# Retention operands 1536 bytes apart, head ends in two parts, and splits moved between engines, in a float32 two-layer trunk

## The chip, the cores and the metric

The kernel runs on one NeuronCore of a Trainium2 chip. The metric is device time in microseconds (us) of one execution; lower is better. Five engines work side by side, each with its own instruction stream, and meet at semaphores: TensorE (PE) multiplies, VectorE (DVE), ScalarE (ACT) and GpSimd (POOL) work on elements, SyncE (SP) issues the weight transfers. PEld is TensorE's weight load.

## The reference

The trunk is two layers over 256 tokens plus 16 meta tokens, so T = 272 columns, with D = 2048:

```python
for layer in range(DEPTH):                       # DEPTH = 2
    u = rmsnorm(h, mix_norm_pre[layer])
    u = hybrid_mixer(u, ...) if layer % 2 == 0 else retention_mixer(u, ...)
    h = h + rmsnorm(u, mix_norm_post[layer])
    u = swiglu(rmsnorm(h, ffn_norm_pre[layer]), w_gate, w_up, w_down)
    h = h + rmsnorm(u, ffn_norm_post[layer])
return h[:, N_META:]

def retention_mixer(h, w_in, w_out):             # 8 heads, q/k 256 wide, v and gate 512 wide
    q, k, v, gate = _split(h @ w_in, RET_IN_SIZES)
    q = _rotate_pairs(q, pos); k = _rotate_pairs(k, pos) * C_QK_DIM ** -0.5
    o = _rms(_chunk_retention(q, k, v))
    return (jax.nn.silu(gate) * o) @ w_out
```

The change touches mostly the product `h @ w_in` of the retention layer and what follows it head by head.

## The kernel before

**Products.** Activations lie transposed: 16 blocks (k) of 128 features in the partitions, tokens along the row. A weight piece is 128 output features times 2048 input features, 1 MB, and gives one output tile. Each float32 number is kept as a high and a low part (`x_hi`, `x_lo`, `w_hi`, `w_lo`, type float32r), and a product of one k is three matmuls, hi·hi, lo·hi and hi·lo, so 48 matmuls a piece. In each of them the weights are the stationary operand (128 by 128) and x is the moving one, 272 columns wide, or 256 where the meta tokens are not needed.

**Making a piece.** SP loads it into `raw` (two slots). ACT copies it to `w_hi` in two halves of 1024 columns (L1501), DVE subtracts to get `w_lo` (L2229, again two halves), and SP may load the slot anew. PE waits for `lo_ready`.

**Where the operands lie.** In bytes from the start of a partition's row, the built program has `x_hi` at 18560, `x_lo` at 35968, `w_hi` at 87200, `w_lo` at 103712, and `mid` and `y_hi` (which share a place) at 143712, `y_lo` at 161120. Weight blocks of successive k are 512 bytes apart. For x there are two layouts, both in `x_of`. With t0 = 0 the rows of successive k are 272 words, 1088 bytes, apart. With t0 = 16, used by the FFN of layer 1, they are 256 words, 1024 bytes, apart and start 56 words (X_FRONT) into the tensor. Retention takes the first layout, also for its pieces of 256 columns, which skip the first 16 words of each row. The activations of the down product of layer 0 lie in `mid`, 2560 bytes apart, the low part 1152 bytes behind the high one (`mid_at`).

**Retention.** `ret_round(i)` is a head: 12 pieces s, q (s = 0, 1; 256 columns), k (2, 3) and v (4 to 7) of 272, gate (8 to 11) of 256. Head 0 is different: its first three pieces are multiplied together while x is still being made (`fresh_three`), all of head 0's first eight with 272 columns. DVE takes each tile out of PSUM; POOL finishes the rotation (L3223, L3224) from `rot_a`. At a head's end `ret_finish` runs on DVE at step s = 0 of the next head: two multiplications of 128 by 1024 (L2984, L2988), then it waits for ACT's high part (L2157), then subtracts the low part (L2994). Only behind these does DVE take tile 0 and split piece 2. Small tensors of the heads (scores, v, gate) are carved out of `u`.

**Openings.** An opening is the start of up0, ret_in and up2 (norms 2, 4 and 6): DVE updates h two blocks at a time (L2314, L2320) and makes `x_lo` (L2305), ACT makes `x_hi`, POOL adds squares (L3075), and PE follows block by block with three pieces at once, of which one sits in `third_hi`/`third_lo` and a fourth waits in `fourth_raw`. Amid the blocks, behind k = 7, DVE also splits the second half of piece 1.

Of the kernel before, what the change touches and what calls it, by code (L numbers as in the profile page):

```python
# [26 lines left out]
F32R = mybir.dt.float32r  # L27
# [4 lines left out]
P = 128  # L32
D = 2048
# [144 lines left out]
def trunk(nc, a, out):  # L178
    ctx = ExitStack()
    st = stage_table()  # L180
    with ctx:
# [7 lines left out]
        h = sb("h", [P, KC, T])  # L189
        x_hi = sb("x_hi", [P, KC, T], F32R)  # L190
# [77 lines left out]
        with ExitStack() as second:  # L268
# [20 lines left out]
            ret_r = sb("ret_r", [P, SEQ], F32, second)  # L289
            ones_ret = sb("ones_ret", [P, P], F32R, second)  # L290
# [23 lines left out]
        sum_hi, sum_lo = third_hi[:, 0:SEQ], third_hi[:, SEQ:2 * SEQ]  # L314
# [4 lines left out]
        def carve(cursor, shape):  # L319

            n = int(np.prod(shape[1:]))
            part = flat[0:shape[0], cursor[0]:cursor[0] + n]
            cursor[0] += n
            assert cursor[0] <= KC * T
# [28 lines left out]
        rel = carve(c4, [P, REL_W])  # L353
        dmask = carve(c4, [P, REL_W])
        ret_s = carve(c4, [P, REL_W])
        v_rows = carve(c4, [P, 2, 512])
        v_tail = carve(c4, [P, 4, 32])
        v_tail_rows = carve(c4, [P, P])
        v_t = carve(c4, [P, T])
        ret_g = carve(c4, [P, 4, SEQ])  # L360
# [135 lines left out]
        def _(sp):  # L496
# [103 lines left out]
            load_third("up2", a["w_up"][4 * HALF + 2])  # L600
            with sp.Fori(0, KC) as i:
                for s in range(2):
                    load(s, FULL, a["w_ret_out"][ds1(2 * i + s)], base + 2 * i + s)
# [27 lines left out]
        def _(pe):  # L631
# [58 lines left out]
            def fresh_hi(norm, k, t0):  # L690
# [3 lines left out]
                mm(o, w_hi[:, 0, k * P:(k + 1) * P], x_of(x_hi, t0)[:, k], k == 0, False)  # L694
                mm(o, w_lo[:, 0, k * P:(k + 1) * P], x_of(x_hi, t0)[:, k], False, False)

            def fresh_lo(norm, k, t0):

                pe.wait_ge(x_lo_ready, KC * (norm // 2) + k + 1)
                return mm(ps[:, BK_0, t0:T], w_hi[:, 0, k * P:(k + 1) * P], x_of(x_lo, t0)[:, k],  # L700
# [29 lines left out]
            def fresh_three(stage, norm, t0):  # L730
# [3 lines left out]
                for k in range(KC + 2):  # L734
# [5 lines left out]
                    if 0 <= j < KC:  # L740
                        if j % 8 == 0:
                            pe.wait_ge(lo_ready, 2 * (base + 1) + 1 + j // 8)
                        pair = multiply(ps[:, BK_1, t0:T], 1, j, 1, lambda _: x_of(x_hi, t0)[:, j],
                                        lambda _: x_of(x_lo, t0)[:, j], j == 0, j == KC - 1)
# [4 lines left out]
                    if n >= 0:  # L749
# [3 lines left out]
                        mm(o, third_hi[:, cut], x_of(x_hi, t0)[:, n], n == 0, False)  # L753
                        mm(o, third_hi[:, cut], x_of(x_lo, t0)[:, n], False, False)
                        last = mm(o, third_lo[:, cut], x_of(x_hi, t0)[:, n], False, n == KC - 1)
# [483 lines left out]
            def mix(n, k0, k1):  # L1239

                piece, _, tile, _ = LAST_AT[f"mix{n}"]
                if k0 == 0:
                    open_tile(piece, tile)
                last = multiply(ps[:, tile % 2, 0:T], piece % 2, k0, k1 - k0, lambda k: y_hi[:, EARLY_K[k0 + k]],
# [20 lines left out]
            gdn_y(g, 1)  # L1265

            pe.wait_ge(FV.sem, FV.after("y_lo", g - 1))
            mix(0, 10, 12)
# [139 lines left out]
            def ret_tile(i, s, t0=0, behind=None):  # L1408
# [5 lines left out]
                multiply(ps[:, s % 2, t0:T], s % 2, 0, KC, lambda k: x_hi[:, k, t0:T], lambda k: x_lo[:, k, t0:T],  # L1414
# [74 lines left out]
        def _(act):  # L1489
# [85 lines left out]
            def fill_x(norm, loaded, after=None):  # L1575
# [3 lines left out]
                def high(k):  # L1579
                    nc.scalar.activation(x_of(x_hi, t0)[:, k], h[:, k, t0:T], ACT.Copy, scale=gains[:, norm, k:k + 1]  # L1580
                                         ).then_inc(x_hi_ready, 1)
# [300 lines left out]
            def mixer_body(i, g, f, d):  # L1882
# [75 lines left out]
                index_pair(i, 14)  # L1958
                index_pair(i, 15)
                gdn_v(g, 2)  # L1960
# [34 lines left out]
            split_last("mix0", EARLY_W, (0,))  # L1995
# [12 lines left out]
            split_last("mix2", EARLY_W)  # L2008
            dsa_exp(5)
            gdn_y(g, 1)  # L2010
# [14 lines left out]
            split_last("mix5", EARLY_W)  # L2025
            dsa_exp(6)
            gdn_y(g, 6)
# [1303 lines left out]
```

## Time and profile before

| | us |
|---|---|
| median of 3 runs | 2899.7 (2899.48 to 2899.88) |
| the profiled execution | 2899.09 |
| its span, first to last instruction | 2897.3 |
| PE busy | 2868.1 (99%) |
| DVE / ACT / POOL busy | 1697.0 / 1367.4 / 233.8 |
| mean granted TensorE clock | 0.999 of full speed |

The span starts with the first instruction of the program; what lies around it is 1.8 us in this execution. A matmul's end is modelled, so its duration reads as 0.28 us while the next one starts after 0.11 to 0.13 us: what a matmul costs here is read from the distance between starts, that is from the length of an unbroken stretch divided by its matmuls. "Idle" of an engine is the time before an instruction in which it did nothing, and the name behind it is what ended that.

### The profile page before, as it was taken

The page shows a single profiled execution, that of the slowest core. Times are in us where ns is not written, and L with a number is a line of the kernel's source. Part 1 is how long each engine was busy: PE and PEld are TensorE (multiplying, and loading weights), DVE is VectorE, ACT ScalarE, POOL GpSimd, SP SyncE. Part 2 cuts the span into 40 slices and gives each one's busy share as a digit, 9 for nine tenths or more (in the row PEclk, how much of TensorE's full clock was granted, in tenths as well). Part 3 has the DMA queues.
Part 4 walks back from the last instruction along what each step waited for, and adds up shares of the span by engine and source line. Part 5 has one row for each costly group of instructions (what it writes and reads, how often), then busy time and mean ns, then how long its engine had stood idle before and what let it go on. Part 6 is the DMA issues. An engine that isn't in the chain of part 4 may idle for free.

```text
span 2897.3 us, 58388 instructions
## 1 busy us (share of the span) xinstructions
PE 2868.1 (99%) x22720; PEld 2796.0 (97%) x22720; DVE 1697.0 (59%) x2404; ACT 1367.4 (47%) x1996; POOL 233.8 (8%) x270
## 2 busy tenths in 40 slices
PE   9999999999999999999999999999999999999998
PEld 8889999999999999999999999999999998899987
DVE  5887775755554555546555555554456556655555
ACT  5556665643333333345544444444454444344443
POOL 2122110200000000001211111110010000000000
PEclk9999999999999999999999999999999999999999
DMA  5222334444445544455444444445544555555554
GB/s 213 102 98 88 124 104 140 163 156 176 176 164 175 183 174 174 176 179 176 145 164 170 165 166 161 169 164 189 190 174 167 193 188 210 196 189 188 189 202 160
DMA packets 74823, 483.89 MB, mean 167 GB/s; under 512 B 8989, under 2 KB 9417, under 8 KB 24432
## 3 DMA queue, kind: packets, MB, share of 16 engines
q1 hardware_dynamic: 74528, 482.30, 46.8%
q8 instruction: 59, 0.97, 0.1%
q0 software_dynamic: 208, 0.39, 0.0%
q14 instruction: 28, 0.23, 0.0%
HBM read 480.41 MB, written 2.10 MB: 167 GB/s over the span
## 4 chain that ended last, share of the span: by engine, by line
PE 90%; DVE 6%; ACT 2%; issue 2%; DMA 0%; POOL 0%; DVEq 0%; SPq 0%; ACTq 0%; POOLq 0%
PE ps L633 89%; DVE w_lo L2378 1%; DVE w_lo L2229 1%; DVE x_lo L2305 1%; DVE ps L2314 0%; DVE h L2320 0%; PE ps L1024 0%; DVE conv_acc L2407 0%; PE ps L1423 0%; ACT w_hi L1501 0%; DMA h<-in_x_t 0%; DVE bias L2509 0%; DVE kq L2421 0%; DVE ret_sq L2988 0%; DVE u L2984 0%
## 5 line engine op out<-in xcount | busy, mean ns | idle before, releaser
L633 PE MATMUL ps<-x_hi,w_hi 128*128 128x272 f32 (+1 forms) x4944 | 1422.4, 288 | 6.7 <-ACT x_hi L1580 3.3
L633 PE MATMUL ps<-x_hi,w_lo 128*128 128x272 f32 (+1 forms) x4944 | 1403.1, 284 | 0.2 <-DVE u L2644 0.2
L633 PE MATMUL ps<-x_lo,w_hi 128*128 128x272 f32 (+1 forms) x4944 | 1400.3, 283 | 2.5 <-DVE x_lo L2305 2.3
L2229 DVE TENSOR_TENSOR w_lo<-raw,w_hi 128x1024 fp32r<-128x1024 f32 (+2 forms) x889 | 1006.9, 1167 | 374.3 <-ACT w_hi L1501 359.5
L1501 ACT ACTIVATE w_hi<-raw 128x1024 fp32r<-128x1024 f32 (+2 forms) x835 | 821.0, 1012 | 506.0 <-PE ps L633 428.3
L633 PEld LDWEIGHTS ps<-x_hi,w_hi 128*128 128x128 f32 x4944 | 931.9, 188 | 14.4 <-issue 6.5
L633 PEld LDWEIGHTS ps<-x_lo,w_hi 128*128 128x128 f32 x4944 | 931.5, 188 | 6.2 <-DVE x_lo L2305 4.9
L633 PEld LDWEIGHTS ps<-x_hi,w_lo 128*128 128x128 f32 x4944 | 927.7, 188 | 0.7 <-DVE u L2644 0.5
L633 PE MATMUL ps<-mid,w_hi 128*128 128x272 f32 (+1 forms) x2432 | 437.1, 282 | 0.0
L633 PEld LDWEIGHTS ps<-mid,w_hi 128*128 128x128 f32 x2432 | 374.3, 188 | 0.0
L633 PE MATMUL ps<-mid,w_lo 128*128 128x272 f32 (+1 forms) x1216 | 342.7, 282 | 0.0
L633 PEld LDWEIGHTS ps<-mid,w_lo 128*128 128x128 f32 x1216 | 227.9, 187 | 0.0
L633 PE MATMUL ps<-w_hi,mid 128*128 128x512 f32 x704 | 218.9, 392 | 0.0
L2119 ACT ACTIVATE mid<-ffn_m 128x272 f32 (+3 forms) x88 | 37.3, 424 | 345.4 <-DVE ffn_m L2956 345.4
L633 PEld LDWEIGHTS ps<-w_hi,mid 128*128 128x128 f32 x704 | 132.0, 188 | 29.5
L2133 ACT ACTIVATE ffn_g<-ffn_g 128x272 f32<-128x272 f32 (+1 forms) x88 | 37.4, 425 | 228.6 <-DVE ffn_g L2944 228.6
L633 PE MATMUL ps<-w_lo,mid 128*128 128x512 f32 x352 | 138.5, 393 | 0.0
L633 PE MATMUL ps<-u 91*91 91x91 f32 (+8 forms) x928 | 110.1, 255 | 3.1 <-DVE state L2649 1.1
L2952 DVE TENSOR_TENSOR ffn_m<-ps,r_pre 128x272 f32<-128x272 f32 (+1 forms) x88 | 38.0, 432 | 124.2 <-PE ps L633 124.2
L633 PEld LDWEIGHTS ps<-u 91*91 91x91 f32 (+4 forms) x928 | 95.9, 158 | 9.5 <-DVE state L2649 1.6
L1548 ACT ACTIVATE sq<-u 128x272 f32<-128x272 f32 (+3 forms) x48 | 20.4, 425 | 145.3 <-DVE u L2354 75.8
L633 PEld LDWEIGHTS ps<-w_lo,mid 128*128 128x128 f32 x352 | 66.1, 188 | 15.3
(362 smaller groups left out, 2355.8 us busy)
## 6 DMA issues: line engine op xcount, KB each, us to landing
raw<-in_w_up SPq DMA_DIRECT2D x172, 1024.0 KB, 4.8
raw<-in_w_ret_in SPq DMA_DIRECT2D x94, 1024.0 KB, 4.8
raw<-in_w_down SPq DMA_DIRECT2D x64, 704.0 KB, 4.0
raw<-in_w_rows SPq DMA_DIRECT2D x44, 1024.0 KB, 4.8
raw<-in_w_heads SPq DMA_DIRECT2D x32, 1024.0 KB, 4.8
raw<-in_w_ret_out SPq DMA_DIRECT2D x32, 1024.0 KB, 4.8
raw<-in_w_mix_early SPq DMA_DIRECT2D x16, 768.0 KB, 4.3
raw<-in_w_latent SPq DMA_DIRECT2D x6, 1024.0 KB, 4.8
```

What stands on the lines that cost most here:

```text
L633: return nc.tensor.matmul(o, lhs, rhs, start=start, stop=stop)
L1501: nc.scalar.activation(w_hi[:, piece % 2, cut], raw[:, piece % 2, cut], ACT.Copy).then_inc(hi_ready, count)
L1548: nc.scalar.activation(sq[:, slot, t0:T], src[:, ds1(k), t0:T], ACT.Square).then_inc(squared, 1)
L2119: nc.scalar.activation(mid[:, bass.ds(mid_at(layer, False, j), w)], ffn_m[:, slot, 0:w], ACT.Copy).then_inc(mid_hi_ready, 1)
L2133: nc.scalar.activation(ffn_g[:, s, 0:w], ffn_g[:, s, 0:w], ACT.Silu).then_inc(gate_silu, 1)
L2229: V.tensor_tensor(w_lo[:, slot, cut], raw[:, slot, cut], w_hi[:, slot, cut], ALU.subtract).then_inc(lo_ready, count)
L2305: V.scalar_tensor_tensor(x_of(x_lo, t0)[:, ds1(k)], h[:, ds1(k), t0:T], gains[:, norm, ds1(k)], x_of(x_hi, t0)[:, ds1(k)], ALU.mult, ALU.s ...
L2378: done = V.tensor_tensor(w_lo[:, s % 2, cut], raw[:, s % 2, cut], w_hi[:, s % 2, cut], ALU.subtract)
L2952: V.tensor_tensor(ffn_m[:, s, 0:w], ps[:, up_bank, t0:T], r_pre[:, t0:T], ALU.mult).then_inc(drained, 1)
```

## The change

1. In retention x has a layout of its own: a tensor `ret_x` over the place of `x_hi`, `x_lo` and `u`, rows of successive k 384 words (1536 bytes) apart, the first at word 40, the low part 16 rows behind. The 272 columns start at byte 18720 + 1536k, the last 256 of them 64 bytes later.
2. What was carved out of `u` for the heads now lies in `h_rows`, the place of `third_hi` and `third_lo`. So the table `rel` is fetched by POOL after the three pieces of the opening, and the third piece of up2 is loaded in the middle of ret_out and no longer at its start.
3. `ret_finish` keeps the two multiplications; the low part is a new `ret_rest`, at s = 1. In head 0 the k tile goes to `rot_b`, in the place of `ret_sq`, and doesn't wait for POOL.
4. In openings POOL subtracts the second half of piece 1 (`split_second`), and no longer DVE. In the first rounds of the FFN, ACT's copy and DVE's split of the piece at slot 1 are made one tile earlier.
5. In the mixer of layer 0 some splits and copies change places, and piece mix0 is made in pieces of 512 and 1024 columns.

```diff
+            ret_x = sb("ret_x", [P, 3 * KC * T], F32R, spaced)
+        RET_FRONT, RET_STEP = 40, 384
-        def x_of(x, t0):
+        def x_of(x, t0, norm=None):
+            if norm == 4:
+                w0 = RET_FRONT + (KC * RET_STEP if x is x_lo else 0)
+                return ret_x[:, w0:w0 + KC * RET_STEP].rearrange("p (c t) -> p c t", c=KC)[:, :, 0:T]
...
-                multiply(ps[:, s % 2, t0:T], s % 2, 0, KC, lambda k: x_hi[:, k, t0:T], lambda k: x_lo[:, k, t0:T],
+                multiply(ps[:, s % 2, t0:T], s % 2, 0, KC, lambda k: x_of(x_hi, 0, 4)[:, k, t0:T],
+                         lambda k: x_of(x_lo, 0, 4)[:, k, t0:T],
...
+            def split_second(stage):
+                piece = st[stage][0] + 1
+                cut = slice(HALF_W, FULL)
+                pool.wait_ge(hi_ready, 2 * piece + 2)
+                pool.wait_ge(lo_ready, 2 * piece + 1)
+                G.tensor_tensor(w_lo[:, 1, cut], raw[:, 1, cut], w_hi[:, 1, cut], ALU.subtract).then_inc(lo_ready, 1)
...
-                        if k == 6:
-                            split_lo(1, FULL, piece, 1)
+                    dve.wait_ge(lo_ready, 2 * piece + 2)
...
-                    if s == 0 and not (isinstance(i, int) and i == 0):
+                    if s == 1 and not (isinstance(i, int) and i == 0):
                         ret_y(i - 1)
...
                     if s == 0 and not first:
                         ret_finish(i - 1)
+                    if s == 1 and not first:
+                        ret_rest(i - 1)
...
+                        to = rot_b if s == 2 and first else rot_a
+                        V.tensor_tensor(to[:, 0, t0:T], tile, rope[:, 0, t0:T], ALU.mult)
...
-                            if not first:
-                                split_next(f"up{n}", i, 4 if opened else 2 * s + 1, 4,
+                            if first:
+                                split_next(f"up{n}", i, 4, 4, FULL)
+                            elif not opened:
+                                split_next(f"up{n}", i, 2 * s + 1, 4,
```

On DVE the turn from one head to the next stood so before (L2229 splits a piece, L2984 and L2988 are the multiplications of `ret_finish`, L2994 the low part, L3020 and L3021 take tile 0):

```order
776 L2984 TENSOR_TENSOR u<-u,ret_r 128x1024
779 L2988 TENSOR_TENSOR ret_sq<-ps,u 128x1024
783 L2994 TENSOR_TENSOR mid<-ret_sq,mid 128x1024
786 L3020 TENSOR_TENSOR rot_a<-ps,rope 128x256
787 L3021 TENSOR_TENSOR rot_a<-ps,rope 128x256
789 L2229 TENSOR_TENSOR w_lo<-raw,w_hi 128x1024
791 L2229 TENSOR_TENSOR w_lo<-raw,w_hi 128x1024
```

and it stands so in the changed kernel (the lines are those of its file):

```order
775 L3023 TENSOR_TENSOR h_rows<-h_rows,ret_r 128x1024
778 L3027 TENSOR_TENSOR ret_sq<-ps,h_rows 128x1024
781 L3063 TENSOR_TENSOR rot_a<-ps,rope 128x256
782 L3064 TENSOR_TENSOR rot_a<-ps,rope 128x256
784 L2258 TENSOR_TENSOR w_lo<-raw,w_hi 128x1024
786 L2258 TENSOR_TENSOR w_lo<-raw,w_hi 128x1024
790 L3034 TENSOR_TENSOR mid<-ret_sq,mid 128x1024
```

The low part, and the wait for ACT before it, moved behind both halves of piece 2.

In the opening of retention DVE stood so before, from the seventh block on (L2305 makes `x_lo`, L2320 and L2314 update h):

```order
720 L2305 SCALAR_TENSOR_TENSOR x_lo<-h,gains,x_hi 128x272 x2
721 L2320 TENSOR_TENSOR h<-h,ps 128x544
722 L2314 TENSOR_TENSOR ps<-u,ps 128x2x272
723 L2229 TENSOR_TENSOR w_lo<-raw,w_hi 128x1024
724 L2305 SCALAR_TENSOR_TENSOR x_lo<-h,gains,x_hi 128x272 x2
```

and now:

```order
720 L2333 SCALAR_TENSOR_TENSOR ret_x<-h,gains,ret_x 128x272 x2
721 L2348 TENSOR_TENSOR h<-h,ps 128x544
722 L2342 TENSOR_TENSOR ps<-u,ps 128x2x272
723 L2333 SCALAR_TENSOR_TENSOR ret_x<-h,gains,ret_x 128x272 x2
724 L2348 TENSOR_TENSOR h<-h,ps 128x544
```

The split of 128 by 1024 is gone from between them; on POOL one of the same size stands ahead of the opening's additions.

In the first rounds of the FFN (here up0; up2 has the same order with 256 columns) DVE stood so before:

```order
516 L2952 TENSOR_TENSOR ffn_m<-ps,r_pre 128x272
517 L2956 TENSOR_TENSOR ffn_m<-ffn_m,ffn_g 128x272
518 L2959 TENSOR_TENSOR mid<-ffn_m,mid 128x272
519 L2944 TENSOR_TENSOR ffn_g<-ps,r_pre 128x272
520 L2229 TENSOR_TENSOR w_lo<-raw,w_hi 128x1024 x2
521 L2952 TENSOR_TENSOR ffn_m<-ps,r_pre 128x272
```

and now:

```order
515 L2989 TENSOR_TENSOR ffn_m<-ps,r_pre 128x272
516 L2993 TENSOR_TENSOR ffn_m<-ffn_m,ffn_g 128x272
517 L2258 TENSOR_TENSOR w_lo<-raw,w_hi 128x1024
518 L2998 TENSOR_TENSOR mid<-ffn_m,mid 128x272
519 L2979 TENSOR_TENSOR ffn_g<-ps,r_pre 128x272
520 L2258 TENSOR_TENSOR w_lo<-raw,w_hi 128x1024
521 L2989 TENSOR_TENSOR ffn_m<-ps,r_pre 128x272
```

One of the two halves that stood ahead of the second `ffn_m` is now made before the low part of the first.

## Rows read from the trace of the kernel before

**Rows 1.** The page: busy time, share of the span, instructions.

```profile
PE 2868.1 (99%) x22720; PEld 2796.0 (97%) x22720; DVE 1697.0 (59%) x2404; ACT 1367.4 (47%) x1996; POOL 233.8 (8%) x270
```

**Rows 2.** The chain in order of time: start us, length us, what, matmuls.

```profile
595.93 763.23 PE ps L633 x6116
...
1404.52 6.00 PE ps L633 x48
...
1410.74 6.01 PE ps L633 x48
...
1416.97 5.69 PE ps L633 x48
```

**Rows 3.** The same view, of ret_out and of the last product of the mixer.

```profile
2007.93 122.17 PE ps L633 x1078
...
503.19 56.22 PE ps L633 x446
```

**Rows 4.** Stretches: PE, PEld, DVE, ACT, POOL busy us (instructions), clock, DMA share, GB/s.

```profile
600.00:700.00 100.00, 100.00 (x802) 100.00 (x801) 54.21 (x69) 38.40 (x50) 0.00 (x0) 1.00 0.49 176
900.00:1000.00 100.00, 100.00 (x804) 100.00 (x804) 48.49 (x62) 38.46 (x48) 0.00 (x0) 1.00 0.53 186
2200.00:2300.00 100.00, 100.00 (x885) 100.00 (x884) 58.76 (x75) 43.36 (x56) 0.00 (x0) 1.00 0.55 197
```

**Rows 5.** A group by shape on PE, 1390 to 2010 us: count, busy us, mean ns, idle.

```profile
L633 PE MATMUL ps<-x_hi,w_hi 128*128 128x256 f32 x736 | 209.0, 284 | 0.0
```

**Rows 6.** PE in order of time: start us, length us, what, [idle before it].

```profile
1532.87 0.28 PE L633 MATMUL ps<-x_hi,w_lo 128*128 128x256 f32 x1
1533.29 0.39 PE L633 MATMUL ps<-x_hi,w_hi 128*128 128x272 f32 x1
1533.51 0.29 PE L633 MATMUL ps<-x_lo,w_hi 128*128 128x272 f32 x1
```

**Rows 7.** DVE in order of time at the same head end.

```profile
1527.44 1.22 DVE L2988 TENSOR_TENSOR ret_sq<-ps,u 128x1024 f32<-128x1024 f32 x1
1530.13 1.22 DVE L2994 TENSOR_TENSOR mid<-ret_sq,mid 128x1024 f32 x1 [1.47 <-ACT mid L2157]
1531.28 0.42 DVE L3020 TENSOR_TENSOR rot_a<-ps,rope 128x256 f32<-128x256 f32 x1
1531.94 2.35 DVE L2229 TENSOR_TENSOR w_lo<-raw,w_hi 128x1024 fp32r<-128x1024 f32 x2
```

**Rows 8.** PE in order of time, around four waits.

```profile
428.28 0.36 PE L633 MATMUL ps<-y_hi,w_hi 128*128 128x272 f32 x1 [0.52 <-issue]
...
1373.60 0.29 PE L633 MATMUL ps<-x_hi,third_lo 128*128 128x272 f32 x1
1374.31 0.39 PE L633 MATMUL ps<-x_lo,w_hi 128*128 128x272 f32 x1 [0.42 <-DVE x_lo L2305]
...
1397.16 0.29 PE L633 MATMUL ps<-x_hi,w_lo 128*128 128x272 f32 x1
1398.06 0.36 PE L633 MATMUL ps<-x_hi,w_hi 128*128 128x272 f32 x1 [0.61 <-DVE k_rot L3025]
...
2192.72 0.28 PE L633 MATMUL ps<-x_hi,w_lo 128*128 128x256 f32 x1
2193.97 0.36 PE L633 MATMUL ps<-x_hi,w_hi 128*128 128x256 f32 x1 [0.98 <-DVE ffn_m L2952]
```

**Rows 9.** Groups by shape on POOL, whole run.

```profile
L3223 POOL TENSOR_TENSOR q_rot<-rot_a,q_rot 128x256 f32<-128x256 f32 x8 | 13.2, 1650 | 149.6 <-DVE q_rot L3025 149.6
L3226 POOL TENSOR_TENSOR ret_sq<-ret_sq 128x512 f32<-128x512 f32 x8 | 10.3, 1282 | 300.8 <-ACT ret_sq L2202 300.8
L3228 POOL TENSOR_TENSOR ret_sq<-ret_sq 128x256 f32<-128x256 f32 x8 | 5.9, 737 | 0.6
```

**Rows 10.** DVE in the opening of retention, in order of time.

```profile
1359.57 1.20 DVE L2229 TENSOR_TENSOR w_lo<-raw,w_hi 128x1024 fp32r<-128x1024 f32 x1
...
1372.62 1.22 DVE L2229 TENSOR_TENSOR w_lo<-raw,w_hi 128x1024 fp32r<-128x1024 f32 x1
```

More of the change, by code:

```diff
@@ L599, in _ @@
             base = st["ret_out"][0]
[L600 to L603, printed above, removed]
+            for i0, i1 in ((0, KC // 2), (KC // 2, KC)):
+                if i0:
+                    sp.wait_ge(RV.sem, RV.after("y", HEADS - 1))
+                    load_third("up2", a["w_up"][4 * HALF + 2])
+                with sp.Fori(i0, i1) as i:
+                    for s in range(2):
+                        load(s, FULL, a["w_ret_out"][ds1(2 * i + s)], base + 2 * i + s)
             ffn(1)
@@ L1994, in _ @@
             table(ACT.Ln)
-            split_last("mix0", EARLY_W, (0,))
+            piece = LAST_AT["mix0"][0]
+            act.wait_ge(piece_in[piece % 2], 16 * (piece // 2 + 1))
+            act.wait_ge(products, SLOT_FREE[piece - 2][0])
+            for c0, done in ((0, quarter_hi), (4 * P, hi_ready)):
+                nc.scalar.activation(w_hi[:, piece % 2, c0:c0 + 4 * P], raw[:, piece % 2, c0:c0 + 4 * P], ACT.Copy
+                                     ).then_inc(done, 1)
             gdn_ln(g)
@@ L2008, in _ @@
             split_last("mix2", EARLY_W)
+            gdn_y(g, 1)
             dsa_exp(5)
-            gdn_y(g, 1)
             dsa_probs(5)
@@ L2773, in _ @@
             dsa_take_q(5)
-            last_lo("mix0", EARLY_W, 0, 1)
+            piece = LAST_AT["mix0"][0]
+            for c0, split, count, done in ((0, quarter_hi, HEADS - LAG + 1, quarter_lo),
+                                           (4 * P, hi_ready, 2 * piece + 1, lo_ready)):
+                cut = slice(c0, c0 + 4 * P)
+                dve.wait_ge(split, count)
+                V.tensor_tensor(w_lo[:, piece % 2, cut], raw[:, piece % 2, cut], w_hi[:, piece % 2, cut], ALU.subtract
+                                ).then_inc(done, 1)
             dsa_take_k(5)
@@ L3014, in ret_round @@
                     if s in (0, 2):
-                        if s == 2:
+                        if s == 2 and not first:
                             dve.wait_ge(RG.sem, RG.after("q", i))
@@ L3212, in square_sum, with ret_round @@
                         add(2 * i + s, s)
+            def split_second(stage):
[4 more added lines that the diff above has]
+                G.tensor_tensor(w_lo[:, 1, cut], raw[:, 1, cut], w_hi[:, 1, cut], ALU.subtract).then_inc(lo_ready, 1)
             square_sum(1)
+            split_second("up0")
             square_fours(2)
             square_sum(3)
+            split_second("ret_in")
             square_fours(4)
-            _, _, tile0 = st["ret_in"]
+            _, sig, tile0 = st["ret_in"]
+            pool.wait_ge(products, sig + 6)
+            pool.dma_start(rel, a["rel"]).then_inc(rel_in, 16)
             G.tensor_copy(ones_ret[:], ones[:])
-            with pool.Fori(0, HEADS) as i:
+            def ret_round(i):
                 for s, (dst, t0) in enumerate(((q_rot, META), (k_rot, 0))):
+                    src = rot_b if s and isinstance(i, int) else rot_a
                     pool.wait_ge(drained, tile0 + 12 * i + 2 * s + 2)
-                    G.tensor_tensor(dst[:, 0], rot_a[:, 0, t0:T], dst[:, 0], ALU.subtract)
-                    G.tensor_tensor(dst[:, 1], rot_a[:, 1, t0:T], dst[:, 1], ALU.add).then_inc(RG.sem, 1)
+                    G.tensor_tensor(dst[:, 0], src[:, 0, t0:T], dst[:, 0], ALU.subtract)
+                    G.tensor_tensor(dst[:, 1], src[:, 1, t0:T], dst[:, 1], ALU.add).then_inc(RG.sem, 1)
                 pool.wait_ge(RA.sem, RA.after("osq", i))
@@ L3232, in _ @@
                 G.tensor_tensor(sum_lo, ret_sq[:, 0], sum_hi, ALU.subtract).then_inc(RG.sem, 1)
+            ret_round(0)
+            with pool.Fori(1, HEADS) as i:
+                ret_round(i)
             square_sum(5)
+            split_second("up2")
             square_fours(6)
```

91 lines of the change are left out of this document (52 added, 39 removed).

## Prediction

> **What bounds the kernel now.** The page comes first: PE is busy in 99% of the span [rows 1]. No engine or transfer beside it can be worth much, so two things are left to find: time that PE sits idle, and time that each matmul takes. For the second the chain in order of time is read, where PE runs without a break, and a stretch is divided by its matmuls. The FFN of layer 0 gives 763.23 / 6116 = 0.1248 us a matmul of 272 columns [rows 2]. Retention gives 6.00 / 48 = 0.1250 for 272 columns, and its first piece of 256 columns 5.69 / 48 = 0.1185 [rows 2]. But ret_out, also 256 columns wide, gives 122.17 / 1078 = 0.1133 [rows 3], and so does the FFN of layer 1: 885 matmuls touch a stretch of 100 us (a row counts those at both edges, so two or three too many), 100 / 882 = 0.1134 [rows 4]. The same width, type and weights cost 0.0052 less there. What differs is where the moving operand lies. The layer 1 FFN and ret_out have every k at the same place modulo 1024 bytes (byte 352 of it), retention has them 1088 bytes apart. The table by shape says the same in its own measure: 284 ns for 256 columns in retention [rows 5].
>
> **Part 1, the layout.** In the changed kernel the last 256 columns of row k start at byte 18784 + 1536k, which is 352 or 864 modulo 1024, so 96 modulo 256 always, as in the fast stretches. Is modulo 256 enough? In the FFN of layer 0 the pitch of 1088 moves x by 64 modulo 256 with each k, and the starts in the trace repeat every 12 matmuls, which is four k's, after which x is back modulo 256 but not modulo 512 or 1024. So I take 0.1133. The pieces of 256 columns are 46 (four in head 0, six in each of the other seven), 46 x 48 = 2208 matmuls, 736 of each of three kinds [rows 5]: 2208 x (0.1185 - 0.1133) = 11.5 us; with the mean of all the 256-column pieces, which I work out at 0.1184 from the starts, 11.2 us. All of it is on PE's own path, with nothing beside it. I take 11.2. Bounds: 0, if the jump of 512 modulo 1024 spoils it, and 11.5.
>
> The 50 pieces of 272 columns, 2400 matmuls, start at 32 modulo 256. No row shows 272 columns at one place for every k, so the price is bounded. From below: the 16 extra columns at the speed of the fast stretches, 0.1133 x 272 / 256 = 0.1204, less than 0.1250 by 0.0046, a gain of 11 us. From above: the last product of the mixer has 272 columns of y, whose places run through 96, 160, 224 and 32 modulo 256, and takes 56.22 / 446 = 0.1261 [rows 3], a loss of 0.0011 x 2400 = 2.6 us. Between them lies the down product of layer 0, high part always at 96, low part at 224 modulo 256, with 100 / 802 = 0.1247 for an edge-corrected stretch [rows 4]: a gain of 0.7 us. That is the nearest row, since there too every k has the same place modulo 256, and yet it is hardly faster than up0 with its wandering place (100 / 800 = 0.1250, [rows 4]). Every 272-wide layout so far costs 0.1247 to 0.1261, whatever its place. I take 0.1248, a gain of 0.5 us.
>
> A word on what is known about such a price. Rows 2 and 3 show two speeds for one width. The Trainium skill, "TensorE: Matmul & The Clock Gate", "Wait — 56ns, not 53.3ns?", gives N / 2.4 GHz and about 2.5 ns, 109 ns for 256 columns and 116 for 272, with no place for an address; "SBUF — State Buffer", "Who interferes with whom", says that PE never waits on anyone. By these the layout would be worth nothing. The traces disagree with both figures (113 to 118, 125) and show the dependence on place.
>
> **Part 2, head ends.** At the turn of a head the last matmul of piece 1 starts at 1532.87 and the first of piece 2 at 1533.29: 0.42 instead of 0.118, and the next 0.22 instead of 0.125 [rows 6], together 0.38 to 0.4 lost; the same pair stands at every one of the seven turns. DVE's rows say why: after ret_sq it stands 1.47 us until ACT's high part, subtracts 1.22, takes tile 0, and only at 1531.94 splits piece 2 [rows 7], whose first half is ready at 1533.2. With the low part behind, tile 0 follows at 1528.7 and the first half is ready near 1530.6, over 2 us before PE wants it; ACT's copies of piece 2 come first too, since its own part moved to s = 1. What is late next: nothing at this turn, the low part itself is wanted only in ret_out. 7 x 0.38 = 2.7 us. In head 0, PE waits for k_rot L3025 and loses 0.90 - 0.125 = 0.77 us [rows 8], since `rot_a` is held by POOL's q; `rot_b` frees it: 0.8 us. The bounds are 0 and these sums.
>
> **Part 3, openings.** In the opening of retention DVE's split at 1372.62 costs 1.22 us in mid-stream [rows 10]; PE shows 0.71 instead of 0.125 between 1373.60 and 1374.31 [rows 8], and 0.24 more two steps on. It doesn't lose the whole 1.2 because DVE has a little lead. Smaller holes of the same kind lie in up0 and up2 (0.5 and 0.5 by the starts): 1.8 us in all. Against it, POOL must now subtract 1024 columns: 256 take 737 ns and 512 take 1282 [rows 9], so 2.4 us by going on at 2.13 ns a column, but 1650 ns for 256 beside a busy DVE, 6.6 us if all of it were so. It begins when DVE has the first half, at about 1360.8 [rows 10], and is wanted at the ninth block, near 1373: even 6.6 us is early enough. But it delays POOL's first sums, and DVE's `x_lo`, which reads two operands from SBUF, can be made to wait. The row of L3223 shows that such pairs hold each other up. The Trainium skill, "SBUF — State Buffer", "Who interferes with whom", says so as a rule: a DVE instruction with two SBUF inputs and a GpSimd one that reads SBUF exclude each other for the whole instruction. By that rule `x_lo` of block 0 stands until POOL ends, near 1363.3, some 0.2 us late. I count 0.3 an opening, 0.9 in all, which leaves 0.9 us; bounds -3 (the DVE chain a microsecond late in each of three openings) and 1.8.
>
> The fourth piece of this part is the largest single wait of PE in the run: 1.25 us between starts at 2192.72, 0.98 of it idle, until ffn_m L2952 [rows 8]; less 0.113 that is 1.14 lost. DVE made both halves of a split before it. With one half and ACT's copy ahead of the first low part, this goes by its 1.2 us of DVE work; up0 has 0.24 of the same. I take 1.2 us of 1.38; bounds 0 and 1.4.
>
> **Part 4, the rest.** In the mixer the exchanges concern holes between 0.2 and 0.5 us, the longest at the start of mix0, 0.52 idle [rows 8], which the split of 512 columns takes up: 0.7 in all, bounds -0.5 and 1.5. `rel` is issued by POOL after the third piece, some 10 us later than before; ACT wants it in step 3 and is not needed by PE before piece 3 ends, so 0. The third piece of up2 loads amid ret_out's pieces (1 MB in about 5 us, and transfers are busy half of the time [rows 4]), wanted 50 us later: 0. The matmuls over `h_rows` in place of `u` are some 25 a head: 0, bounds -0.5 and 0.5.
>
> **The sum** from the profiled execution, 2899.09 (2897.3 of span and 1.8 around it): 11.2 + 0.5 + 2.7 + 0.8 + 0.9 + 1.2 + 0.7 = 18.0, so 2881.1; the median of the runs lies 0.6 above that execution, so 2881.7. I say 2882.
>
> **The rivals.**
> A, the forecast: 256 columns at the fast price, 272 as ever. For it: two stretches of the fast layout, four slow ones of 272. 2882, own range 2878 to 2886. Chance 0.52.
> B, the steady place makes 272 columns fast too, at 0.1204 or near. For it: at the pitch of 1088 both widths pay nearly the same above their columns (0.1184 - 0.1067 and 0.1250 - 0.1133 are both 0.0117), so perhaps both lose it; against it: the steady down product of layer 0. 11 us more than A less the 0.5: 2871.5. Chance 0.22. Half way, 0.122, it would be 2876: chance 0.13.
> C, the layout does nothing, since what makes the fast stretches fast is the pitch of exactly 1024 and not the place modulo 256: only parts 2 to 4, 6.3 us: 2893.4. For it: no row has 1536. Chance 0.08.
> D, slower than before: a pitch of 1536 is worse than 1088, for both widths. Place: all 4608 matmuls of ret_in. If each costs as much more as y's stretch does over 0.1248, 0.0013, that is 6 us and parts 2 to 4 just pay for it; it is slower from 0.0014 a matmul on, and with twice y's excess, 0.0026, it is 12.0 - 6.3 = 5.7 us slower: 2905.5. Chance 0.03.
> E, the openings turn: POOL's subtraction holds up DVE's chain by 1 us in each, and nothing else changes from A: 2885, inside A's range; chance 0.02 apart from A.
>
> **Numbers.** A range that leaves out no more than 2 in 10 reaches from B to the upper edge of A: 2870 to 2889. What this kernel's measurement can tell from no change is 0.2%, 5.8 us. Faster by more than that: A, B, half of C's spread and E, 0.92; within it: the rest of C and a little of D, 0.05; slower: 0.03.
>
> **What would show it.** In the changed profile, piece by piece on the chain: 5.44 us for 48 matmuls of 256 columns in ret_in (C: 5.69), 6.00 for 272 (B: 5.78). At the head turns the starts of PE 0.12 apart where they were 0.42, and DVE's low part behind piece 2. No 0.7 in the opening of retention and no 1.25 at the start of up2; POOL's 128 by 1024 between 2.4 and 6.6 us. The prediction is wrong if retention's matmuls of 256 columns are not at 0.113, or if those of 272 move from 0.125 by more than 0.001.

## The result

The changed kernel takes 2884.14 us (median of 5, 2883.84 to 2886.08), the kernel before 2899.70 (median of 5): a ratio of 0.9948, with a 95% interval of 0.9937 to 0.9959. The forecast was 2882 with a range of 2870 to 2889. The executions that were profiled took 2883.84 and 2899.09 us, with spans of 2882.0 and 2897.3. Their last matmuls lie 15.25 us apart, and it can be said where this was gained: both programs issue 22720 matmuls in the same order, so the start of one matmul in the one trace, less the start of the matmul of the same number in the other, says how much was gained up to there:

| stretch (times of the changed kernel) | gained, us | foretold for it |
|---|---|---|
| mixer, to 547 us | 2.34 | 0.7 |
| opening and first round of up0, to 601 us | -0.53 | about 0.4 |
| rest of layer 0 | 0 | 0 |
| opening and first pieces of retention, to 1402 us | 1.66 | 0.5 + 0.8 |
| pieces of retention, to 1985 us | 10.11 | 11.7 + 2.7 |
| ret_out | 0 | 0 |
| opening of up2 | 0.45 | 0.2 |
| its first round | 1.23 | 1.0 |
| the rest, to the end | 0 | 0 |

The page of the changed kernel still has PE at 99%, 12.6 us shorter in busy time than in [rows 1]. Below it the chain, retention in head 0 (start us, length us, what, matmuls):

```profile
PE 2855.5 (99%) x22720; PEld 2787.2 (97%) x22720; DVE 1694.7 (59%) x2402; ACT 1370.3 (48%) x1997; POOL 239.3 (8%) x273
```

```profile
1401.04 6.06 PE ps L647 x48
...
1407.32 6.07 PE ps L647 x48
...
1413.61 5.50 PE ps L647 x48
```

Against [rows 2] the piece of 256 columns went from 5.69 to 5.50, not quite to the 5.44 that was foretold, and the two of 272 went up, from 6.00 and 6.01 to 6.06 and 6.07, where no change was foretold. The table by shape of the same stretch as [rows 5] (`ret_x` now stands for the high and the low part, so each row counts both) has 278 ns for 256 columns where it had 284:

```profile
L647 PE MATMUL ps<-ret_x,w_hi 128*128 128x272 f32 x1465 | 279.6, 290 | 0.0
L647 PE MATMUL ps<-ret_x,w_hi 128*128 128x256 f32 x1472 | 255.0, 278 | 0.0
```

Worked out from start to start, over all pieces and without the steps that hold a pause, a matmul of 256 columns costs 0.1139 us (before 0.1184) and one of 272 costs 0.1262 (before 0.1251).

At the head end of [rows 6, 7], DVE in order of time and then PE (start us, length us, what, idle before it in brackets):

```profile
1522.02 1.22 DVE L3027 TENSOR_TENSOR ret_sq<-ps,h_rows 128x1024 f32<-128x1024 f32 x1
1523.16 0.41 DVE L3063 TENSOR_TENSOR rot_a<-ps,rope 128x256 f32<-128x256 f32 x1
1523.49 0.41 DVE L3064 TENSOR_TENSOR rot_a<-ps,rope 128x256 f32<-128x256 f32 x1
1523.82 2.35 DVE L2258 TENSOR_TENSOR w_lo<-raw,w_hi 128x1024 fp32r<-128x1024 f32 x2
1526.09 1.21 DVE L3034 TENSOR_TENSOR mid<-ret_sq,mid 128x1024 f32 x1
```

```profile
1526.97 0.28 PE L647 MATMUL ps<-ret_x,w_lo 128*128 128x256 f32 x1
1527.09 0.42 PE L647 MATMUL ps<-ret_x,w_hi 128*128 128x272 f32 x2
```

No idle stands after `ret_sq`, the split begins at 1523.82 with both its halves, and only then comes the low part into `mid`. PE goes from the one piece to the next in 0.12 us.

The opening of up0 is the one place that got slower. DVE, GpSimd (POOL) and PE there:

```profile
558.82 0.73 DVE L2342 TENSOR_TENSOR ps<-u,ps 128x544 f32<-128x544 f32 x1
559.46 2.55 DVE L2333 SCALAR_TENSOR_TENSOR x_lo<-h,gains,x_hi 128x272 fp32r<-128x272 f32 x2
```

```profile
558.43 2.36 POOL L3261 TENSOR_TENSOR w_lo<-raw,w_hi 128x1024 fp32r<-128x1024 f32 x1 [5.87 <-ACT w_hi L1522]
560.75 0.96 POOL L3120 TENSOR_TENSOR ffn_g<-ffn_g 128x272 f32<-128x272 f32 x1
```

```profile
559.68 0.28 PE L647 MATMUL ps<-x_hi,w_lo 128*128 128x272 f32 x1
561.14 0.39 PE L647 MATMUL ps<-x_lo,w_hi 128*128 128x272 f32 x1 [1.18 <-DVE x_lo L2333]
...
563.25 0.39 PE L647 MATMUL ps<-x_hi,w_hi 128*128 128x272 f32 x1 [0.79 <-ACT x_hi L1601]
```

GpSimd's split runs from 558.43 to 560.79, 2.36 us, what was worked out (2.4). DVE's first `x_lo` starts in the middle of it and ends at 561.09, 0.30 us after it. The second starts at 561.01, beside GpSimd's addition, which lasts to 561.71, and ends at 562.01, again 0.30 us after it. So the pair takes 2.55 us. PE then waits 1.18 us for the first, and 0.79 us more for ACT, which DVE's next update of h reached late.

### The profile page after: what moved, and what is told of

Same layout as the page of the kernel before. It is cut to its first block, busy times and chain, and to the rows that moved or that the text cites. A ratio compares the mean times of both kernels' runs of the same rounds, so it can differ in the third digit from the quotient of the medians.

```text
span 2882.0 us, 58385 instructions
## 1 busy us (share of the span) xinstructions
PE 2855.5 (99%) x22720; PEld 2787.2 (97%) x22720; DVE 1694.7 (59%) x2402; ACT 1370.3 (48%) x1997; POOL 239.3 (8%) x273
## 4 chain that ended last, share of the span: by engine, by line
PE 94%; DVE 4%; ACT 1%; issue 1%; DMA 0%; SPq 0%; DVEq 0%; ACTq 0%
PE ps L647 93%; DVE w_lo L2406 1%; PE ps L1038 0%; DVE conv_acc L2435 0%; PE ps L1444 0%; DVE w_lo L2258 0%; DMA h<-in_x_t 0%; DVE bias L2537 0%; DVE x_lo L2333 0%; DVE kq L2449 0%; DVE ps L2342 0%; DVE h L2348 0%; ACT w_hi L2002 0%; DVE top L2548 0%; DVE p_t L2550 0%
## 5 line engine op out<-in xcount | busy, mean ns | idle before, releaser
L647 PE MATMUL ps<-x_hi,w_hi 128*128 128x272 f32 (+1 forms) x3424 | 985.5, 288 | 4.5 <-ACT x_hi L1601 3.1
L647 PE MATMUL ps<-x_lo,w_hi 128*128 128x272 f32 (+1 forms) x3424 | 969.1, 283 | 3.1 <-DVE x_lo L2333 2.9
L647 PE MATMUL ps<-x_hi,w_lo 128*128 128x272 f32 (+1 forms) x3424 | 970.3, 283 | 0.2 <-DVE u L2672 0.2
L647 PEld LDWEIGHTS ps<-x_hi,w_hi 128*128 128x128 f32 x3424 | 645.5, 189 | 9.0 <-issue 3.0
L647 PEld LDWEIGHTS ps<-x_lo,w_hi 128*128 128x128 f32 x3424 | 645.3, 188 | 6.0 <-DVE x_lo L2333 4.7
L647 PEld LDWEIGHTS ps<-x_hi,w_lo 128*128 128x128 f32 x3424 | 642.4, 188 | 0.6 <-DVE u L2672 0.5
L647 PE MATMUL ps<-ret_x,w_hi 128*128 128x272 f32 (+1 forms) x3040 | 555.9, 284 | 0.7 <-ACT ret_x L1601 0.7
L647 PEld LDWEIGHTS ps<-ret_x,w_hi 128*128 128x128 f32 x3040 | 469.1, 188 | 1.6 <-ACT ret_x L1601 0.7
L647 PE MATMUL ps<-ret_x,w_lo 128*128 128x272 f32 (+1 forms) x1520 | 430.3, 283 | 0.0
L647 PEld LDWEIGHTS ps<-ret_x,w_lo 128*128 128x128 f32 x1520 | 286.3, 188 | 0.0
```

Of the source, the lines that this page charges most:

```text
L647: return nc.tensor.matmul(o, lhs, rhs, start=start, stop=stop)
```

## The experiments

Each is the changed kernel with the edit shown. "Against the changed kernel" means the same comparison of starts, matmul by matmul, between one execution of each; it is given for a stretch, so that a difference elsewhere in the run stays out of it. The kernel before took 2899.59 to 2899.65 us beside all of them.

### The layout undone, and other places

```diff
-        RET_FRONT, RET_STEP = 40, 384
+        RET_FRONT, RET_STEP = 0, 272
```

> The changed kernel with one thing undone: in retention the rows of the normalized input lie 1088 bytes apart again, from the place they had before; all else as changed. My theory: the layout is worth what the trace of the changed kernel shows against the one of before, 2208 matmuls of 256 columns at 0.1139 instead of 0.1184 (9.9 us) less 2400 of 272 columns at 0.1262 instead of 0.1251 (2.7 us), so 7.2 us: this kernel takes 2884.1 + 7.2 = 2891.3 us, its 256 columns are back at 0.1184 and its 272 at 0.1251. Rival: the slower 272 columns come from something else in the change (the copies over other memory, the moved low parts); then they stay at 0.1262 here and the time is 2894.0. Second rival: the 256 columns are faster for another reason than their place; then the time stays near 2884 to 2887.

Measured: 2892.81 us (11 runs, 2891.23 to 2894.16), 8.7 above the changed kernel. Its pieces:

```profile
1403.29 6.02 PE ps L647 x48
...
1409.54 6.01 PE ps L647 x48
...
1415.77 5.69 PE ps L647 x48
```

The old lengths of [rows 2] are back, 0.1184 and 0.1251 from start to start, and the retention pieces are 7.59 us longer than in the changed kernel. The theory said 7.2 and named both prices. The first rival falls, since 272 columns come down too, and the second, since the time is not near 2884. The execution in the trace is 9.8 us longer than the changed kernel's; what is not in retention lies in the first 60 us (0.73) and in the opening of up0 (1.44, told below).

Four kernels keep the pitch of 1536 and move the first row, one keeps the place modulo 256 and changes the pitch (`RET_FRONT, RET_STEP` = 0, 384; 8, 384; 24, 384; 56, 384; and 40, 320):

> The changed kernel with the rows of the normalized input still 1536 bytes apart, but all moved: 272 columns start at 128 modulo 256 for every k and the last 256 columns at 192. Theory P (place): what counts is the place modulo 256, and 96 is a good one for 256 columns; elsewhere 256 columns cost up to 0.118, and 272 columns change too, somewhere in 0.120 to 0.130. Theory S (steadiness): any place is good for 256 columns if it is the same for every k: 256 stays at 0.1133 to 0.1139 and 272 at 0.126, 2884. The time is 2884.1 + 2208 x (256's price - 0.1139) + 2400 x (272's price - 0.1262).

> As the last, with 272 columns at 160 modulo 256 and the last 256 columns at 224. Theory P: another price for at least one of the widths. Theory S: the same prices as in the changed kernel, 0.1139 and 0.1262, 2884.

> As the last, with 272 columns at 224 modulo 256 and the last 256 columns at 32. Theory P: another price for at least one of the widths. Theory S: the same prices as in the changed kernel, 0.1139 and 0.1262, 2884.

> As the last, with 272 columns at 96 modulo 256 (where the high part of the down product of layer 0 has them, at 0.1247) and the last 256 columns at 160. Theory P: 272 columns at about 0.1247 or lower, 256 columns anywhere from 0.113 to 0.118; with 0.118 for them the time is 2884.1 + 9 - 3.6 = 2889.5, with 0.113 it is 2880. Theory S: 0.1139 and 0.1262, 2884.

> The changed kernel with the rows 1280 bytes apart, so the last 256 columns still start at 96 modulo 256, but at four places modulo 1024 instead of two. Theory: the place modulo 256 is all that counts: 256 columns at 0.1139, 272 at 0.1262, 2884.1. Rival: the place modulo 512 or 1024 counts too: 256 columns above 0.1145 and the time above 2885.5.

| pitch | place of 272, of 256 (modulo 256) | us a matmul of 272, of 256 | retention pieces, against the changed kernel | median, us |
|---|---|---|---|---|
| 1536 | 32, 96 (the changed kernel) | 0.1262, 0.1139 | 0 | 2884.14 |
| 1280 | 32, 96 | 0.1262, 0.1139 | -0.02 | 2885.89 |
| 1536 | 96, 160 | 0.1245, 0.1191 | 7.93 | 2892.19 |
| 1536 | 128, 192 | 0.1256, 0.1187 | 9.50 | 2894.56 |
| 1536 | 160, 224 | 0.1250, 0.1174 | 5.38 | 2890.80 |
| 1536 | 224, 32 | 0.1256, 0.1183 | 8.50 | 2893.10 |
| 1088 | four places in turn | 0.1251, 0.1184 | 7.59 | 2892.81 |

A piece of 272 columns and one of 256 at 96 and 160; then the same at 160 and 224, with a later piece of 256 below; then of the pitch of 1280:

```profile
1401.38 5.98 PE ps L647 x48
...
1413.78 5.71 PE ps L647 x48
```

```profile
1402.69 6.05 PE ps L647 x48
...
1415.23 5.45 PE ps L647 x48
...
1491.14 5.71 PE ps L647 x48
```

```profile
1403.04 6.07 PE ps L647 x48
...
1415.61 5.50 PE ps L647 x48
```

Theory S, that any steady place is good, falls: one place for all k's is not enough, four of five such places leave 256 columns at 0.117 to 0.119. What counts is the place modulo 256, since the pitch of 1280, with other places modulo 1024, has the very same prices. (Its median is 1.8 us higher all the same; in its trace 1.46 us of that lie in the opening of up0, where the granted clock fell, as told below, and none in retention.) Of the places tried, 96 is the good one for 256 columns, and for 272 too, where it gives 0.1245; but the 272 columns of a row start 64 bytes ahead of its last 256, so both can't have it in this form. At 224 a piece of 256 columns takes about 5.45 in some cases and 5.71 in others in the same kernel, and a piece mostly keeps the spacing that it has at its start, so the 0.1174 there is a mean of two. What decides between them is not shown.

### The head ends in one part, at both layouts

```diff
                     if s == 0 and not first:
                         ret_finish(i - 1)
-                    if s == 1 and not first:
                         ret_rest(i - 1)
...
-                    if s == 1 and not (isinstance(i, int) and i == 0):
+                    if s == 0 and not (isinstance(i, int) and i == 0):
                         ret_y(i - 1)
```

> The changed kernel with the end of a head in one part again: the copy of y's high part by ScalarE and the low part by VectorE stand in the first step of the next head, ahead of the split of the next piece. My theory: PE loses 0.38 us at each of seven head turns, 2.7 us: 2886.8 us. Rival: the wait was covered elsewhere by now (the pieces of 256 columns are faster, so PE comes to piece 2 earlier), and it costs more: PE is 0.5 us earlier at the turn in this kernel, so up to 7 x 0.9 = 6 us, 2890. Second rival: nothing, 2884.1.

Measured: 2890.30 us, 5.94 us of it in retention against the changed kernel, 0.85 at each of seven turns. The theory of 2.7 us falls, and the rival with up to 0.9 a turn is right. PE at the turn, and DVE before it:

```profile
1527.82 0.28 PE L647 MATMUL ps<-ret_x,w_lo 128*128 128x256 f32 x1
1528.71 0.51 PE L647 MATMUL ps<-ret_x,w_hi 128*128 128x272 f32 x2 [0.62 <-DVE w_lo L2258]
```

```profile
1522.86 1.23 DVE L3027 TENSOR_TENSOR ret_sq<-ps,h_rows 128x1024 f32<-128x1024 f32 x1
1525.56 1.23 DVE L3034 TENSOR_TENSOR mid<-ret_sq,mid 128x1024 f32 x1 [1.47 <-ACT mid L2184]
1526.70 0.42 DVE L3062 TENSOR_TENSOR rot_a<-ps,rope 128x256 f32<-128x256 f32 x1
1527.03 0.41 DVE L3063 TENSOR_TENSOR rot_a<-ps,rope 128x256 f32<-128x256 f32 x1
1527.37 2.35 DVE L2258 TENSOR_TENSOR w_lo<-raw,w_hi 128x1024 fp32r<-128x1024 f32 x2
```

DVE is the same 1.47 us late as in [rows 7]; PE arrives sooner, so 0.89 lies between two starts where [rows 6] had 0.42. If that is so, 0.4 us must lie between the starts again once the columns are slow again:

> The changed kernel with two parts undone together: the rows 1088 bytes apart from their old place, and the head ends in one part. Theory I (the two interact: PE waits at a head turn for a low part whose time VectorE sets, and comes to it 0.43 us earlier with the faster 256 columns): at the old layout the turn costs 0.4 us as in the kernel before, so this kernel is 7 x 0.4 = 2.8 us behind the one with the old layout alone, which took 2892.8: 2895.6. Theory A (the parts add): 6.0 us behind it as at the new layout, 2898.8.

Measured: 2895.33 us (10 runs). Its turn:

```profile
1531.43 0.28 PE L647 MATMUL ps<-ret_x,w_lo 128*128 128x256 f32 x1
1531.85 0.39 PE L647 MATMUL ps<-ret_x,w_hi 128*128 128x272 f32 x1
```

It is 0.42 again, and there are 2.54 us more in the retention pieces than with the old layout alone. Theory I, that the two parts work on each other, is right. The four kernels beside each other (retention pieces against the changed kernel): with both parts 0, with the layout alone 5.94, with the head ends alone 7.59, with neither 10.13. The kernel before stands at 10.11, so these two parts are all of the gain in the retention pieces. The layout alone is worth 10.13 - 5.94 = 4.2 us, the head ends alone 2.5, both together 10.1.

### GpSimd's split

In all three openings undone, and in up0 alone:

```diff
+                        if k == 6:
+                            split_lo(1, FULL, piece, 1)
-                    dve.wait_ge(lo_ready, 2 * piece + 2)
...
-            split_second("up0")
...
-            split_second("ret_in")
...
-            split_second("up2")
```

> The changed kernel with the second half of the second piece's low part back on VectorE, in the middle of its chain, in all three openings; GpSimd splits nothing. My theory: the opening of up0 was made 0.5 us slower by GpSimd's split, those of retention and up2 0.8 and 0.4 us faster; so this kernel is 0.7 us slower than the changed one, 2884.8, with PE's hole at the eighth block back in all three. Rival: the two engines exclude each other at no net cost and the gain comes from the split alone: 1.8 us slower, 2885.9. Second rival: the changed kernel's splits by GpSimd are worth nothing in sum: 2884.1.

```diff
+                        if k == 6 and norm == 2:
+                            split_lo(1, FULL, piece, 1)
-                    dve.wait_ge(lo_ready, 2 * piece + 2)
+                    if norm != 2:
+                        dve.wait_ge(lo_ready, 2 * piece + 2)
...
-            split_second("up0")
```

> The changed kernel with GpSimd's split taken out of the opening of up0 alone (VectorE makes it at the seventh and eighth block there, as before); retention and up2 keep it. My theory: in up0 one low part of VectorE stood 2.55 us instead of 0.9 while GpSimd's split ran, and this goes; PE's two idle stretches of over 1 us behind it go back to 0.3 and 0.7, its hole at the eighth block comes back, net 0.5 us faster: 2883.6. Rival: the long low part is VectorE waiting for something else (the high part of its block, by ScalarE); then it stays long and the time is 2884.4 or more, since VectorE has the split besides.

Measured: 2884.42 us without any of them, 2883.37 us (2882.83 to 2883.55) with the two in retention and up2. Against the changed kernel the first is 0.45 faster in up0, 0.70 slower in retention's opening and 0.45 slower in up2's, close to the 0.5, 0.8 and 0.4 that were foretold before it ran. The second is 0.93 faster in up0, with the same code there as the first; the half microsecond between them is a fall of the clock in the first, told below. DVE and PE of the second, at the place of the 2.55:

```profile
559.51 0.91 DVE L2336 SCALAR_TENSOR_TENSOR x_lo<-h,gains,x_hi 128x272 fp32r<-128x272 f32 x2
```

```profile
559.74 0.28 PE L647 MATMUL ps<-x_hi,w_lo 128*128 128x272 f32 x1
560.07 0.39 PE L647 MATMUL ps<-x_lo,w_hi 128*128 128x272 f32 x1
...
561.66 0.39 PE L647 MATMUL ps<-x_hi,w_hi 128*128 128x272 f32 x1 [0.44 <-ACT x_hi L1601]
```

With no GpSimd instruction beside it the pair takes 0.91. So it was GpSimd that held it, by its split and the addition right behind, and not ACT's high part. In the changed kernel the line by itself reads (durations in ns, least, median, most):

```profile
L2333 DVE SCALAR_TENSOR_TENSOR x_lo<-h,gains,x_hi x8: 487/496/1629, 559.5 to 568.4; 128x272 fp32r<-128x272 f32 x8
```

So the one that met the split took 1.13 us longer than the usual one, and the one behind it, which met the addition, 0.50. The Trainium skill, "SBUF — State Buffer", "Who interferes with whom", gives the rule: a DVE instruction with two inputs from SBUF and a GpSimd instruction that reads SBUF exclude each other, and the one issued later is blocked until the other is through. The traces agree: both `x_lo` end 0.30 us after the GpSimd instruction that they met, while L2342, which reads one operand from SBUF and one from PSUM, takes 0.73 us at 558.82 beside the split, as it does without it. In retention's opening the split lasts from 1359.10 to 1361.47 and `x_lo` begins at 1361.33: the pair takes 0.91 there, and the split costs nothing. In up2 the split lasts to 2148.02, `x_lo` (256 columns) begins at 2147.51 and takes 0.79 us where the next takes 0.47, and PE is 0.32 us later by 2148 than without the split.

This version, with GpSimd splitting in two openings of three, has the lowest median of all (ratio to the kernel before 0.9943, interval 0.9930 to 0.9957). All five of its runs lie below all five of the changed kernel, but those were timed in another series, and the 0.8 us between the medians lie inside the intervals.

There may be a second cost. In the kernel with the old layout, what follows the two pauses of PE in the opening of up0 (PE, PEld, DVE, ACT, POOL busy, granted clock, DMA share, GB/s):

```profile
560.00:564.50 4.50, 2.31 (x14) 1.65 (x13) 4.39 (x6) 2.21 (x7) 2.60 (x2) 1.00 0.66 213
564.50:568.00 3.50, 3.50 (x19) 3.50 (x18) 3.40 (x7) 2.21 (x6) 1.23 (x2) 0.53 0.38 159
```

and in the version with two splits:

```profile
564.50:568.00 3.50, 3.50 (x30) 3.50 (x29) 3.30 (x7) 2.09 (x7) 2.19 (x3) 1.00 0.00 0
```

PE is never idle in the stretch from 564.50, but the granted clock is 0.53 of full, that is, mostly at the level of 1.2 GHz, and 19 matmuls are counted where 30 were: 1.44 us. It fell after PE had been idle for about half of the 4.5 us before. Of the 11 profiled executions of kernels with GpSimd's split in up0, five show it behind these pauses (1.31 to 1.46 us each), and six, the changed kernel's own among them, have the same pauses at the full clock. Of the three kernels without that split two show no fall. The third, with no split by GpSimd at all, shows one a little earlier:

```profile
556.00:560.00 4.00, 4.00 (x22) 3.74 (x22) 1.63 (x4) 2.86 (x7) 0.00 (x0) 0.63 0.98 414
```

Ahead of it PE had not been idle, but had made matmuls of 1 and of 128 columns for three microseconds. The version with two splits, with the same code there, has the full clock in this stretch, and by the end of the opening the two differ by 0.48 us. So the clock can fall in this opening without GpSimd's split, and that the split makes the fall likelier or dearer is argued, not shown: five of 11 against one of three. Such a fall is a likely reason for the changed kernel's run of 2886.08, and for part of the difference between the medians above and the sums by stage; no trace shows it for those runs. The Trainium skill, "TensorE: Matmul & The Clock Gate", "What's actually happening", says that the clock follows how busy the engine has been and that the point of the switch varies. The traces agree in so far as the same pauses were followed by a fall in some executions and not in others, and the fall began at points between 563.2 and 564.7 us.

### The exchanges undone

In the mixer (mix0's first split in one piece, copies, rows and splits in their old order):

```diff
-            mix(0, 10, 11)
...
-            mix(0, 11, 12)
+            mix(0, 10, 12)
...
-            for c0, done in ((0, quarter_hi), (4 * P, hi_ready)):
-                nc.scalar.activation(w_hi[:, piece % 2, c0:c0 + 4 * P], raw[:, piece % 2, c0:c0 + 4 * P], ACT.Copy
-                                     ).then_inc(done, 1)
+            split_last("mix0", EARLY_W, (0,))
...
+                take_tile(i, 2)
                 gdn_state(g, 0)
-                take_tile(i, 2)
...
```

> The changed kernel with the exchanges in the mixer undone (the first split of mix0 in one piece of 512 columns, and the copies, rows and splits in their old order). Theory: all that the stage up to 499 us gained (2.6 us between the two traces) comes from them: 2886.7. Rival (my prediction's term): 0.7 us, the rest was a difference between two executions: 2884.8.

Measured: 2887.26 us, 2.72 us in the mixer (without its first 60 us, where executions differ from one to the next). The theory holds. PE's waits between 110 and 173 us, first of this kernel, then of the changed one (waiting line, whom for, us in total, times, longest):

```profile
PE ps L647 <- ACT dsa_s L1765: 1.8, 3, 1.1
PE ps L647 <- ACT v_new L1873: 1.2, 1, 1.2
PE ps L647 <- DVE state L2666: 1.1, 1, 1.1
...
PE ps L647 <- POOL third_hi L3177: 0.3, 1, 0.3
```

```profile
PE ps L647 <- ACT dsa_s L1771: 2.3, 4, 1.1
PE ps L647 <- DVE state L2677: 0.8, 1, 0.8
PE ps L647 <- DVE state L2679: 0.7, 1, 0.7
```

The wait of 1.2 us for ACT's v_new goes, and some of it returns as a longer wait for dsa_s (1.8, now 2.3): 0.86 net at that place. Between 425 and 500 us there are 1.5 more, and the remaining 0.4 has no one place. The exchanges were undone together, so which of them gives what is not shown.

In the FFN (both halves of the fifth piece's low part ahead of DVE's first product, ACT's copies behind it):

```diff
-                            if first:
-                                split_next(f"up{n}", i, 4, 4, FULL)
-                            elif not opened:
-                                split_next(f"up{n}", i, 2 * s + 1, 4,
+                            if not first:
+                                split_next(f"up{n}", i, 4 if opened else 2 * s + 1, 4,
...
-                            elif opened:
-                                split_lo(1, FULL, st[f"up{n}"][0] + 5, 1)
...
-                            if first:
-                                split_lo(1, FULL, st[f"up{n}"][0] + 5, 0, 1)
```

> The changed kernel with the exchange in the first rounds of the two FFN layers undone (both halves of the fifth piece's low part ahead of VectorE's first product there, ScalarE's copies behind it). Theory: PE's wait of about 1.2 us at the start of up2 comes back, and 0.2 in up0: 2885.5. Rival: with the second piece's split gone from the opening VectorE is earlier there and half of the wait is covered: 2884.7.

Measured: 2885.41 us; 1.25 of it in the first round of up2 and 0.30 in up0. The theory holds, and its rival falls. The wait of [rows 8] is back:

```profile
2179.04 0.28 PE L647 MATMUL ps<-x_hi,w_lo 128*128 128x256 f32 x1
2180.30 0.36 PE L647 MATMUL ps<-x_hi,w_hi 128*128 128x256 f32 x1 [0.98 <-DVE ffn_m L2985]
```

## Why the prediction was right, and where its terms were not

The mechanism and the order of the terms were right: retention's layout and the waits of its head ends first, and no engine but PE sets the end. The sum was 18.0 and the traces show 15.25. One of the prediction's own signs of being wrong did come: matmuls of 272 columns moved from 0.125 by more than 0.001, to 0.1262, and with them it took the one term with the wrong sign. The other, 256 columns not at 0.113, came out at the edge, with 0.1139. By its steps:

- **256 columns, 11.2 us.** Measured 2208 x (0.1184 - 0.1139) = 9.9. Place modulo 256 is enough, as taken. What was missed: 0.1133 is the price once a piece has settled. In 24 of the 46 pieces the first twenty of the 48 matmuls take 0.1151 to 0.1161 in the mean, in the others 0.1133 or 0.1134. The stretch of ret_out, from which the price was read, has no such slow starts in its mean; why these pieces have them is not shown.
- **272 columns, 0.5 us gained.** This is the term that failed: 2400 x (0.1262 - 0.1251) = 2.6 us were lost. Of three rows that of the down product was taken as the nearest, because its place is steady. But steadiness is not what counts, and the down product's high part lies at 96, where 272 columns do cost 0.1245. The row of y [rows 3], with 0.1261, was the right end of the bounds by number; its places include 32 once in four. That the layout paid all the same rests on the 256 columns alone.
- **Head ends, 2.7 us.** At the old layout 2.5 by the runs. But in the sum they did more than their own: without them, the layout's 7.6 would have shrunk to 4.2, because PE's earlier arrival would have been waited away at each turn. The sum took the two terms apart and came out right only because both were in the change. That nothing is late next was right.
- **rot_b, 0.8 us.** The opening and first pieces of retention gained 1.66, of which GpSimd's split made 0.70. Of the 0.96 that are left, 0.77 come in one step between 1392 and 1395 us, where PE had waited for k_rot and no longer does. `rot_b` was not undone by itself.
- **Openings, 0.9 us net.** By the runs at the full clock -0.93 in up0, +0.70 in retention and +0.45 in up2: 0.2, inside the bounds of -3 to 1.8. The price of exclusion was sized by one case: 0.3 an opening was 0 in retention and 0.3 in up2, but 1.6 in up0, where DVE's instruction came 1.0 us after GpSimd's began and the next one met GpSimd's addition. There PE was 1.65 us late by 565 us, and the hole that the split had made before gave back only 0.7.
- **First rounds of the FFN, 1.2 us.** 1.25 + 0.30 when undone, 0.2 more than the 1.38 of the rows.
- **Mixer, 0.7 us.** 2.3 between the traces, 2.7 when undone. The term counted the pauses at mix0, which gave 0.2, and passed over the exchanges in the rounds before and in the later mix pieces: 0.9 net between 140 and 173 us, 0.7 near 470 and 0.6 near 495.

So there were 1.3 and 3.1 us too much for the columns and 0.9 too much for up0, some 1.6 too little for the mixer, and the rest lies within half a microsecond. That the time came out only 2.1 us above the 2882 is in part luck: what the mixer gave beyond its term covers half of the 3.1 us.

The rivals: B (272 columns at 0.1204) and C (only a pitch of 1024) fall by the places tried: nothing gives 272 columns less than 0.1245, and pitches of 1280 and 1536 are alike. D had half of its ground, since 272 columns did rise by 0.0011, but not 256. E was right in size in up0, where the changed kernel's DVE chain came over 1 us late, by 0.3 in up2, and not in retention.

## What to carry to other kernels

When PE is busy 99% of the time, read the time of one matmul stage by stage before looking for waits: one width had two prices here, and moving the operand's start modulo 256 bytes was worth about as much as all the waits that were removed. But try the places, width by width, since the good one can't be read off the steadiness of the layout; and when an engine is made faster, add the waits that it will meet sooner, by testing each part with and without the other. Work given to GpSimd should not begin just ahead of a VectorE instruction on the critical chain that reads two operands from SBUF.

## What the runs showed of the hardware

- 256 float32 columns cost 0.1139 us a matmul at 96 modulo 256 bytes and 0.1174 to 0.1191 at 32, 160, 192 and 224; 272 columns 0.1245 at 96, 0.1250 at 160, 0.1256 at 128 and 224, 0.1262 at 32. Why 96 is good stays open: the place of the weights was not moved.
- At 224, pieces of 48 matmuls in one kernel take about 5.45 us or 5.71 us.
- In the opening of up0, after two pauses of PE of 1.2 and 0.8 us, the granted clock was mostly at the level of 1.2 GHz for the next few microseconds in five of 11 executions (1.31 to 1.46 us lost), and at the full clock in six. Once, in a kernel without these pauses, it fell in the same opening behind matmuls of 1 and 128 columns.
- GpSimd subtracts 128 x 1024 float32 in 2.36 to 2.37 us, beside a DVE that is busy, and a DVE instruction of 0.5 us that met it took 1.63. One that began 0.14 us before GpSimd's end took no longer than usual, and one that began 0.51 us before it took 0.3 longer.
